# Two sequences, one pass over a shared layer's weights

## The reference, cut

```python
for i in range(DEPTH):                       # 2 layers
    m, mc = adaln(c, ...), adaln(c_ctx, ...) # modulation rows
    h  = half_ffn(h,  m,  0, ..., ffn_w_in[i, 0], ffn_w_out[i, 0])
    hc = half_ffn(hc, mc, 0, ..., ffn_w_in[i, 0], ffn_w_out[i, 0])
    u, uc = modulated_norm(h, ...), modulated_norm(hc, ...)
    y, yc = mixer(u, uc, ...)                # attention; x also sees the context's keys and values
    h = gated_residual(h, y, ...)
    h = half_ffn(h, m, 6, ..., ffn_w_in[i, 1], ffn_w_out[i, 1])
    if i < DEPTH - 1:                        # the context needs no more behind its last keys
        hc = gated_residual(hc, yc, ...)
        hc = half_ffn(hc, mc, 6, ..., ffn_w_in[i, 1], ffn_w_out[i, 1])

def swiglu_2(h, w_in, w_out):                # inside half_ffn; 2816 hidden features
    gate, up = jnp.split(h @ w_in, 2, axis=-1)
    return (jax.nn.silu(gate) * up) @ w_out
```

## Time and profile before

| | |
|---|---|
| time, median of 3 runs (lowest, highest) | 2665.64 us (2664.68, 2666.6) |
| the profiled execution's own time | 2669.68 us |
| its span, first to last instruction | 2667.9 us |
| mean granted TensorE clock | 0.976 |
| PE, DVE, ACT busy | 2509.9, 1691.3, 1250.0 us |
| bytes read from HBM | 471.48 MB, 177 GB/s |

### The profile page before, as it was taken

How to read it: one execution, slowest core, us unless ns; L and a number is a source line. 1 busy time by engine, 2 the same in 40 slices (tenths; PEclk the granted TensorE clock), 3 DMA queues, 4 the chain that set the end, 5 groups by cost and what they waited for, 6 DMA issues and landing times.

```text
span 2667.9 us, 48974 instructions
## 1 busy us (share of the span) xinstructions
PE 2509.9 (94%) x20876; PEld 2379.4 (89%) x20876; DVE 1691.3 (63%) x2794; ACT 1250.0 (47%) x1697; POOL 1.2 (0%) x6
## 2 busy tenths in 40 slices
PE   6899998999999999999898999999999999887998
PEld 6799997888998899988887999999999999766997
DVE  5756575656766564566777667576665567656555
ACT  5444453454444444445445555454444345435443
POOL 0000000000000000000000000000000000000000
PEclk9899999999999999999998999999999999898999
DMA  6366656334556655654352344555545555363553
GB/s 223 142 244 242 254 185 220 127 118 147 186 205 235 231 213 205 223 212 167 128 193 80 113 154 164 181 180 175 189 170 179 190 170 183 126 229 139 177 180 119
DMA packets 71591, 480.14 MB, mean 180 GB/s; under 512 B 8784, under 2 KB 9296, under 8 KB 17744
## 3 DMA queue, kind: packets, MB, share of 16 engines
q1 hardware_dynamic: 66240, 468.74, 49.8%
q10 hardware_dynamic: 5136, 8.28, 1.0%
HBM read 471.48 MB, written 1.05 MB: 177 GB/s over the span
## 4 chain that ended last, share of the span: by engine, by line
PE 73%; DVE 14%; ACT 7%; DMA 3%; issue 3%; ACTq 0%; DVEq 0%
PE bank L265 64%; ACT whi L224 4%; DVE wlo L244 3%; DVE wlo L231 2%; PE bank L1144 2%; DMA raw<-w_main 1%; PE bank L1027 1%; DMA raw<-w_down 1%; PE bank L965 1%; DVE ARX L716 1%; DVE HX L662 1%; DVE tmpx L656 1%; PE bank L1015 1%; DMA tmpx<-ARX 0%; PE bank L1710 0%
## 5 line engine op out<-in xcount | busy, mean ns | idle before, releaser
L265 PE MATMUL bank<-HNX_hi,whi 128*128 128x256 f32 x2968 | 860.1, 291 | 43.0 <-DVE wlo L244 17.3
L224 ACT ACTIVATE whi<-raw 128x2048 fp32r<-128x2048 f32 (+1 forms) x378 | 705.3, 1868 | 309.1 <-PE bank L265 155.6
L231 DVE TENSOR_TENSOR wlo<-raw,whi 128x1024 fp32r<-128x1024 f32 (+1 forms) x378 | 453.4, 1199 | 624.9 <-ACT whi L224 623.9
L265 PE MATMUL bank<-HNX_hi,wlo 128*128 128x256 f32 x2968 | 844.7, 286 | 0.0
L265 PE MATMUL bank<-HNX_lo,whi 128*128 128x256 f32 x2968 | 830.5, 285 | 0.0
L265 PEld LDWEIGHTS bank<-HNX_hi,whi 128*128 128x128 f32 x2968 | 577.2, 194 | 68.5 <-issue 37.9
L265 PEld LDWEIGHTS bank<-HNX_hi,wlo 128*128 128x128 f32 x2968 | 577.7, 195 | 0.0
L265 PEld LDWEIGHTS bank<-HNX_lo,whi 128*128 128x128 f32 x2968 | 569.0, 194 | 1.3 <-issue 1.1
L244 DVE TENSOR_TENSOR wlo<-raw,whi 128x1024 fp32r<-128x1024 f32 (+1 forms) x378 | 451.1, 1193 | 0.0
L265 PE MATMUL bank<-HNC_hi,whi 128*128 128x256 f32 x1344 | 390.6, 291 | 9.6 <-DVE tmpc L468 5.7
L265 PE MATMUL bank<-HNC_hi,wlo 128*128 128x256 f32 x1344 | 382.0, 284 | 0.0
(11 more groups left out here) (347 smaller groups left out, 2788.5 us busy)
## 6 DMA issues: line engine op xcount, KB each, us to landing
raw<-w_main SPq DMA_DIRECT2D x270, 1024.0 KB, 4.8
raw<-w_ada SPq DMA_DIRECT2D x72, 1024.0 KB, 4.8
raw<-w_down SPq DMA_DIRECT2D x72, 1024.0 KB, 4.9
raw<-w_down SPq DMA_DIRECT2D x36, 768.0 KB, 4.2
raw<-w_cmp SPq DMA_DIRECT2D x4, 1024.0 KB, 5.5
tmpx<-ARX ACTq DMA_DIRECT2D x18, 128.0 KB, 5.5
tmpx<-ARX ACTq DMA_DIRECT2D x32, 64.0 KB, 4.7
HX<-x_in SPq DMA_DIRECT2D x2, 512.0 KB, 5.9
```

What stands on the lines that cost most here:

```text
L224: NS.activation(WHI[q % HIS][:, 0:size], RAW[m % SLOTS][:, 0:size], ACT.Copy).then_inc(sems["w_hi"], 1)
L231: NV.tensor_tensor(WLO[m % SLOTS][:, 0:half], RAW[m % SLOTS][:, 0:half], WHI[q % HIS][:, 0:half].bitcast(fp32), SUB)
L265: return NT.matmul(dst, (WHI[ordinal[n] % HIS], WLO[n % SLOTS])[w][:, k * 2 * P + col:k * 2 * P + col + P], x[xp][:, kx, :], start=start, ...
```

## The change

The layer gu4 is done in one pass for both sequences, as far as that goes. The context does its first four pairs alone with their four down blocks, as before (`ffn` with `parts`), and then waits. x does the first two blocks (pair 0) alone. Pairs 4 to 10 are then done for both: the activations of both lie in one tensor `BOTH`, and a product's moving operand is 2 x 256 columns, x's and the context's, from two places of it (`of_both`); the result fills a whole bank, x's half and the context's. Pairs 4 to 6 and 7 to 10 are two groups, each with four down blocks of both (6 and 8 feature tiles), the first behind pair 7, the second behind x's pair 1. The second closes the context's layer. Then x does pairs 2 and 3 and the down blocks of its own four pairs; there the two additions to `X.Y` stand ahead of the `put_out` of both tiles, and one block behind.

Besides: the context may go on in gu1 up to its keys (`c_keys` for `ffn00`); its `ga_in` waits for the end of x's gu4 (`x_gu4`) and no longer for x's first attention, and the norm ahead of it has a pitch of 2.5 instead of 6; in the very first norm the high half of the first split stands ahead of the root, and the silu of the modulation's input behind the norm; modulation blocks of the last attention split one block ahead, not two.

```diff
+        def of_both(at_x, at_c):
+
+            whole = BOTH[:, :]
+            return bass.AP(tensor=whole.tensor, offset=whole.offset + at_x, ap=[list(whole.ap[0]), [at_c - at_x, 2], [1, T]])
...
-            def splits(n, last=False, most=None, apart=False, reach=3):
...
+                if high_only:
+                    return
...
+            def product(dst, n, col, k, x, xp, kx, w, start, stop, loose=False, both=None):
...
-                                 x[xp][:, kx, :], start=start, stop=stop, skip_group_check=loose)
+                                 both(xp, kx) if both else x[xp][:, kx, :], start=start, stop=stop, skip_group_check=loose)
...
-            def ffn(S, which, gain, first):
...
-                chunks = [range(0, 4), range(4, 8), range(8, 11)] if S.chunked else [range(0, 11)]
+                chunks = parts or ([range(0, 4), range(4, 8), range(8, 11)] if S.chunked else [range(0, 11)])
...
+                if parts:
+                    summed_c.update({mp: held["y", mp] for mp in range(4)})
+                    passed.add(f"c_at{which}")
+                    while f"both{which}" not in passed:
+                        yield ("W",)
...
+            def ffn_of_both(which, gain_x, gain_c, first, alone, groups):
...
+                GATES, UPS = (BANK[0], BANK[1]), (BANK[2], BANK[3])
...
+                def both_pair(p):
+
+                    kept = (TMPC, TMPX)[(p - alone) % 2]
+                    for b, banks in enumerate((GATES, UPS)):
+                        yield ("D",)
+                        n = take("x", "w_main", base + 2 * p + b)
+                        on(pe, *(free.get(bank.name) for bank in banks))
+                        tile = up("x_tile")
+                        yield from two_tiles(X, n, [bank[:, :].rearrange("p (a b) -> p a b", a=2) for bank in banks], None, ALL, True, True,
+                                             None, tile, both=normed_of_both)
+                        if b == 0:
+                            silu(banks, kept, (tile, done(n)))
+                        else:
+                            keep(banks, kept, (tile, done(n)), both_tiles(p))
+
+                def down(k0, k1, mp, banks, dsts, x, slots, both=None, behind=()):
+
+                    cuts = (k0, k1) if k1 - k0 <= 8 else (k0, (k0 + k1) // 2, k1)
+                    for a, b in zip(cuts, cuts[1:]):
+                        yield ("D",)
+                        n = take("x", "w_down", (4 * which + mp, a * 2 * P), (b - a) * 2 * P)
+                        if a == k0:
+                            on(pe, *(free.get(bank.name) for bank in banks))
+                        waits = {slots[k]: [lo_marks[k]] for k in range(a, b)} if mp == 0 else None
+                        tile = up("x_tile") if b == k1 else None
+                        yield from two_tiles(X, n, dsts, x, [(k - a, slots[k]) for k in range(a, b)], a == k0, b == k1, waits, tile, both=both)
+                        if a == k0:
+                            for job in behind:
+                                job()
+                    return tile, done(n)
+
+                def both_down(pairs, opening, closing):
+
+                    k0, k1 = 2 * pairs[0], 2 * pairs[-1] + 2
+                    same = {k: k for k in range(k0, k1)}
+                    for mp in range(4):
+                        banks = (GATES, UPS)[mp % 2]
+                        ready = yield from down(k0, k1, mp, banks, [bank[:, :].rearrange("p (a b) -> p a b", a=2) for bank in banks], None, same,
+                                                lambda xp, k: gated_of_both(xp, x_slot[k], c_slot[k]))
+                        for m, (bank, mark) in enumerate(zip(banks, ready)):
+                            k, copied, added = 2 * mp + m, up("act_step") if opening else None, up("dve_step")
+                            if opening:
+                                if on(act, mark, *free.get(("x", "dst"), ())):
+                                    NS.activation(X.Y[:, k, :], bank[:, 0:T], ACT.Copy).then_inc(copied.sem, 1)
+                                if dve:
+                                    dve.wait_ge(*copied)
+                                    dve.wait_ge(*summed_c[mp])
+                                    NV.tensor_tensor(C.Y[:, k, :], C.Y[:, k, :], bank[:, T:2 * T], ADD).then_inc(added.sem, 1)
+                            elif dve:
+                                dve.wait_ge(*mark)
+                                dve.wait_ge(*held["y", k])
+                                NV.tensor_tensor(X.Y[:, k, :], X.Y[:, k, :], bank[:, 0:T], ADD)
+                                NV.tensor_tensor(C.Y[:, k, :], C.Y[:, k, :], bank[:, T:2 * T], ADD).then_inc(added.sem, 1)
+                            free[bank.name] = held["y", k] = added
+                            if closing:
+                                put_out(C, C.Y[:, k, :], k, gain_c, added)
+
+                yield ("F",)
...
+                first_blocks(X, n, X.pair, *first)
+                silu(X.pair[:1], TMPX[:1], (done(n),))
+                keep(X.pair[1:], TMPX[:1], (done(n + 1),), x_tiles(0))
+                want(f"c_at{which}")
+                late = None
+                for g, pairs in enumerate(groups):
+                    for p in pairs:
+                        yield from both_pair(p)
+                        if late is not None:
+                            yield from both_down(late, True, False)
+                            late = None
+                    late = pairs
+                yield from x_pair(1)
+                flush()
+                yield from both_down(late, len(groups) == 1, True)
+                passed.add(f"both{which}")
+                for p in range(2, alone):
+                    yield from x_pair(p)
+                flush()
+                pending = ()
+                for mp in range(4):
+                    banks = X.tiles[2 * (mp % 2)], X.tiles[2 * (mp % 2) + 1]
+                    ready = yield from down(0, 2 * alone, mp, banks, [bank[:, 0:T] for bank in banks], X.G, x_slot, behind=pending)
+
+                    def close(mp=mp, banks=banks, ready=ready):
+                        sums = []
+                        for m, (bank, mark) in enumerate(zip(banks, ready)):
+                            k, added = 2 * mp + m, up("dve_step")
+                            if dve:
+                                dve.wait_ge(*mark)
+                                dve.wait_ge(*held["y", k])
+                                NV.tensor_tensor(X.Y[:, k, :], X.Y[:, k, :], bank[:, 0:T], ADD).then_inc(added.sem, 1)
+                            free[bank.name] = added
+                            sums.append(added)
+                        for m in range(2):
+                            k = 2 * mp + m
+                            put_out(X, X.Y[:, k, :], k, gain_x, sums[m])
+                    pending = (close,)
+                close()
 
 
...
+                if opening:
+                    splits(-1, most=1, high_only=True)
                 inv = inverse_root(S, known, hh, rms_h, now(f"{t}_total"))
                 if then is not None:
                     table_of(then)
-                if opening and on(act, in_vec):
-                    NS.activation(CCOL[:, :, 6:8], vec("c").rearrange("p (k s) -> p k s", s=2), ACT.Silu).then_inc(silu_c.sem, 1)
...
+                if opening and on(act, in_vec):
+                    NS.activation(CCOL[:, :, 6:8], vec("c").rearrange("p (k s) -> p k s", s=2), ACT.Silu).then_inc(silu_c.sem, 1)
...
-                    splits(n, reach=2 if "ga" in passed else 3)
+                    splits(n, reach=1 if "ga" in passed else 3)
...
-                        if can("c", "D", "d") and not ("ffn00" in passed and urge[0] == 1):
+                        if can("c", "D", "d") and not ("c_keys" in passed and urge[0] == 1):
...
-                yield from ffn(X, 4, post(X, 1, 0), x)
+                yield from ffn_of_both(4, post(X, 1, 0), post(C, 1, 0), x, 4, (range(4, 7), range(7, 11)))
+                passed.add("x_gu4")
...
+                passed.add("c_keys")
...
-                yield from ffn(C, 4, post(C, 1, 0), x)
+                yield from ffn(C, 4, post(C, 1, 0), x, (range(0, 4),))
...
-                x = yield from norm(C, True, pre(C, 1, 1), [now("c_evac")], mods)
-                while "x_da" not in passed:
+                x = yield from norm(C, True, pre(C, 1, 1), [now("c_evac")], mods, pitch=2.5)
+                while "x_gu4" not in passed:
                     yield ("W",)
```

## The result

The changed kernel takes 2675.3 us (median of nine runs, 2671.03 to 2679.26), the kernel before on the same chip 2667.4 us (2664.68 to 2669.71): 1.0029 times as long, with a 95% interval of 1.0021 to 1.0038. It is slower by 0.3%, where 2634 us (2616 to 2648) and a gain of 1.2% had been forecast. The profiled execution is the one of 2675.3 us, with a span of 2673.6 us; that of the kernel before (2669.7 us) was 2.3 us over its median, so the two profiles lie 5.7 us apart and the medians 7.9.

What follows compares the result with a forecast made beforehand. TensorE (PE), busy 94% of the span, was taken as the bound. Terms -24.2 + 5.4 - 16 - 2 + 11 - 5 - 1 = -31.8 us gave a span of 2636.1, a median of 2634 us (2616 to 2648).

Steps and rivals of the forecast that it cites:

- The products of both: Merged gate, up and down products of gu4: 1008 products 512 columns wide at 216 ns, -24.2 us (-27 to 0).
- The context's keys earlier: Context some 25 to 27 us ahead: first shared attention -16 us (-19 to -8), x's norm ahead of da_in -2 us.
- Late next: Norm ahead of gu4: context out of work two blocks before x's down ends, norm stands bare, +11 us (+8 to +15).
- New waits in the merged layer: Three places in the merged gu4 lose the context block that lay in between, together +5.4 us (+2 to +10).
- (a): After the first two blocks, the first wide gate needs both of their banks: a wait of 2.4 us.
- (b): After pair 1, the wide down needs the bank that pair 1's up has just filled: 1.9 us.
- (c): After pair 3, x's own down waits at its seventh tile for the halves of the pair's product: 1 us.
- Behind the merged layer: x's own down crowded on DVE, but two context ga_in blocks inside x's next norm: -5 us (-10 to +3).
- (A): Rival: columns are the price, a wide product takes 240 ns and merging gives nothing; 2658 us, chance 0.11.
- (C): Rival: reading columns from two distant runs of memory costs, at 260 ns a product 2678 us, slower; chance 0.06.
- the 2655 us: Time by the Trainium skill's rule, N/2.4 + 2.5 ns per warm product, by which merging would save 2.6 us.
- (B): Rival: a wait eats the context's 27 us lead, attention begins bare, gu4's norm is bare too; 2650 us, chance 0.14.

## Why the prediction was wrong

**The products of both.** The term was mis-sized: 227 ns, not 216, so 13 us, not 24. The step that failed is "most of the 120 ns is there whatever the width, and a wider product covers it". The floor of 0.10 us read from one-column products is a floor, not a part that is added. At half clock a product has no surcharge over its columns, and I carried that to full clock. What the three widths show is a constant 13.5 ns at any width, nothing that a wider product hides: merging two products saves that constant once. The range for this term (-27 to 0) held it, but it was wide enough to hold nearly every answer.

**The context's keys earlier.** Attention's start is right: -14.0 for -16, and PE's waits at the transposes are gone. The step that failed is what follows on "this norm is over before attention begins": nothing was written down for where it would be instead. It lay in x's da_in and in the norm ahead of it. There PE had been waiting little, and the two cost 12.5 us together where I had -2; the third and fourth layer lost 6.8 more. I had moved a cost and counted only its old place. The run with the keys alone shows it (15 us off at attention, 12 on at these two places), and the one with the steps 6 apart shows that da_in's part is the context's norm. In x's norm ahead of da_in PE's added loss sits mostly where it waits for DVE's steps of the context's head norm (2.3, 1.2 and 1.9 us, from 1280 to 1289 us in the kernel after); no run takes these steps away.

**Late next.** That the norm ahead of gu4 would stand bare was right: 6.5 us in it and 1.9 in the first blocks behind it, against 11. The run without the keys shows that, with the merged layer, the keys made it so; with the keys and the slower norm behind da_out it is covered as well.

**New waits in the merged layer.** (a) 2.5 us for 2.4, (b) 1.1 for 1.9, (c) 0.3 for 1: right.

**Behind the merged layer.** The place was named: additions behind the context's norm, PE waiting at the third block. The size failed: own down loses 13.8 us (0.3 of it is (c)), and the three stages behind give back 5.8, +7.7 in all for -5. Two steps were off. I counted DVE's work as if it ran without a break, 36.5 us to x's totals; it took 43.6 (2246.66 to 2290.2 us), with DVE waiting in between for splits that ACT held behind the context's tiles. And I counted the two ga_in blocks as cover in x's norm. They stand ahead of x's own small products in PE's queue, and from the first one's start to the second's are 9.7 us: its 48 products are unbroken, but its eviction comes late (the line at 2293.23 us above). So x's totals, ready at 2290.2, came to PE at 2297.8, and the norm with 11.5 us of work in it lost nearly what it had lost bare: 13.0 for 14.3.

**Sum.** Wide products +11, da_in and its norm +14.5, behind the merged layer +12.7, layers three and four +6.8, attention +2; less 2.6 at gu4's norm, 1.5 in the new waits and some 4 of scatter ahead of the second layer: 39 us, where 37.9 lie between the forecast of -31.8 and the ledger's +6.1. **The rivals:** (A) and (C) fall with the 227 ns, though that lies as near to (A)'s 240 as to my 216; the 2655 us, which rest on a constant of 2.5 ns and a saving of 2.6 us, fall too, as the steps give 13 us; (B) isn't what happened, as attention did start covered. The case that came isn't among them: the waits were moved to places that were full before. The 0.09 for slower, the side that came, was too little, because every term with a plus sign was held to the wait that I could name.

## What to carry to other kernels

When work is moved off a bare place, price it at its new place as well: list what is queued behind it there on each engine, above all weight splits and evictions. Merging two passes removes only what a product costs beyond its columns, here 13.5 of 120 ns, and takes from the scheduler the blocks that lay between; check that what becomes ready only at the end of the merged part (here a norm of 12 us on DVE) still has other blocks beside it. A block put into a wait covers it only if its own splits and evictions come in time, for all that stands behind it in the queue waits with it.

## What the runs showed of the hardware that was not expected

A product of split f32 weights at full clock starts 13.5 ns later than its columns need, for 256, 384 and 512 columns alike (120.1, 173.5, 227.0 ns), and reading the 512 columns from two distant runs costs nothing (227 ns either way). At half clock the same 256 columns start 213 ns apart, just their columns, so the constant shows only at full clock. Where it comes from no run here tells.
